# One set of 128 slots for two experts of different router groups, and eight landing slots for the weights

## The reference, cut to what matters

```python
N_GROUPS, EXPERTS_PER_GROUP, TOP_K, D_FF_EXPERT = 4, 4, 2, 512     # 16 experts

def moe(h2, router_w, router_b, w1, w3, w2):
    scores = jax.nn.sigmoid(h2 @ router_w)
    biased = (scores + router_b).reshape(n_tok, N_GROUPS, EXPERTS_PER_GROUP)
    group_score = jnp.sum(lax.top_k(biased, 2)[0], axis=-1)
    gidx = jnp.argmax(group_score, axis=-1)            # one group for each token
    _, loc = lax.top_k(in_group, TOP_K)                # two experts of that group
    eid = gidx[:, None] * EXPERTS_PER_GROUP + loc
    gates = sel / jnp.sum(sel, axis=-1, keepdims=True)
    ...
    y = (jax.nn.silu(xb @ w1[e]) * (xb @ w3[e])) @ w2[e]     # for the tokens of expert e
    return y * g[:, None]                                    # and summed back to the tokens
```

## Time and profile before

| | |
|---|---|
| median of 3 runs | 2137.87 us (2137.78 to 2141.77) |
| the profiled execution | 2146.0 us, span 2144.2 us |
| granted TensorE clock, mean | 0.952 |
| PE busy | 93% of the span |
| DVE, ACT busy | 67%, 53% |
| read from memory | 454.35 MB, 212 GB/s over the span |
| first mixture layer | about 250 to 608 us of the span |
| second mixture layer | about 753 to 1110 us of the span |

### The profile page before, as it was taken

The page is one execution under the profiler, slowest core; times in us unless marked ns, Lnnn a source line. Parts: engine busy times, 40 slices in busy tenths (PEclk is TensorE's granted clock), DMA queues, the critical chain, the costliest instruction groups (busy, mean ns, idle before and its releaser), DMA issues.

```text
span 2144.2 us, 28128 instructions
## 1 busy us (share of the span) xinstructions
PE 1995.2 (93%) x11557; PEld 1698.1 (79%) x11557; DVE 1431.9 (67%) x1851; ACT 1136.8 (53%) x1499; POOL 79.6 (4%) x84
## 2 busy tenths in 40 slices
PE   4984899999989899999979999989999999989998
PEld 2843688888767678888869998779999998778997
DVE  2666588888776588888866555656556556666555
ACT  3332477676657467676745445535344443645433
POOL 0000001000000010010000000000000000000000
PEclk8987899999989899999989999979999999989999
DMA  8563688888759558787855555325555555424552
GB/s 319 197 229 144 216 294 293 296 294 295 275 181 322 205 199 307 282 307 283 305 200 177 183 190 192 118 80 180 193 181 175 195 179 191 156 80 152 181 194 91
DMA packets 209328, 457.33 MB, mean 213 GB/s; under 512 B 8848, under 2 KB 20776, under 8 KB 209192
## 3 DMA queue, kind: packets, MB, share of 16 engines
q1 hardware_dynamic: 204800, 450.99, 60.1%
q10 hardware_dynamic: 4392, 4.44, 0.6%
HBM read 454.35 MB, written 1.05 MB: 212 GB/s over the span
## 4 chain that ended last, share of the span: by engine, by line
PE 87%; DVE 6%; ACT 4%; DMA 2%; issue 1%; POOL 0%; SPq 0%; ACTq 0%; DVEq 0%; POOLq 0%
PE bank L290 84%; PE bank L1906 2%; DVE arena L1206 2%; DVE rest L618 1%; DMA raw<-in_mod_w 1%; ACT round L601 1%; PE bank L2165 1%; DVE arena L1198 1%; ACT arena L727 0%; DMA raw<-in_ev_out_w 0%; DMA raw<-in_od_in_w 0%; DVE acc L1198 0%; DVE xres L1198 0%; PE bank L2147 0%; DVE htokl L1198 0%
## 5 line engine op out<-in xcount | busy, mean ns | idle before, releaser
L618 DVE TENSOR_TENSOR rest<-raw,round 128x1024 fp32r<-128x1024 f32 (+1 forms) x760 | 889.7, 1217 | 266.3 <-ACT round L601 265.5
L601 ACT ACTIVATE round<-raw 128x1024 fp32r<-128x1024 f32 (+1 forms) x760 | 758.6, 1050 | 415.1 <-PE bank L290 389.4
L290 PE MATMUL bank<-hTh,round 128*128 128x256 f32 x1600 | 451.0, 282 | 15.2 <-DVE hTl L1198 12.8
L290 PE MATMUL bank<-hTh,rest 128*128 128x256 f32 x1600 | 449.9, 281 | 0.0
L290 PE MATMUL bank<-hTl,round 128*128 128x256 f32 x1600 | 448.7, 280 | 0.0
L290 PEld LDWEIGHTS bank<-hTh,round 128*128 128x128 f32 x1600 | 302.6, 189 | 21.6 <-issue 20.9
L290 PEld LDWEIGHTS bank<-hTl,round 128*128 128x128 f32 x1600 | 303.7, 190 | 1.1 <-issue 0.2
L290 PEld LDWEIGHTS bank<-hTh,rest 128*128 128x128 f32 x1600 | 303.2, 189 | 0.0
L290 PE MATMUL bank<-round,hTh 128*128 128x512 f32 x464 | 188.1, 405 | 6.5 <-DVE hTl L1198 2.9
L290 PE MATMUL bank<-rest,hTh 128*128 128x512 f32 x464 | 184.2, 397 | 0.0
L290 PE MATMUL bank<-round,hTl 128*128 128x512 f32 x464 | 184.1, 397 | 0.0
(11 more groups left out here) (219 smaller groups left out, 2543.4 us busy)
## 6 DMA issues: line engine op xcount, KB each, us to landing
raw<-in_ex_w SPq DMA_DIRECT2D x192, 1024.0 KB, 5.6
raw<-in_mod_w SPq DMA_DIRECT2D x48, 1024.0 KB, 7.3
raw<-in_ffn_w_gate SPq DMA_DIRECT2D x44, 1024.0 KB, 5.0
raw<-in_ffn_w_up SPq DMA_DIRECT2D x44, 1024.0 KB, 5.0
raw<-in_ffn_w_down SPq DMA_DIRECT2D x44, 1024.0 KB, 4.8
raw<-in_w_in SPq DMA_DIRECT2D x20, 1024.0 KB, 5.0
raw<-in_ev_in_w SPq DMA_DIRECT2D x10, 1024.0 KB, 9.9
raw<-in_od_in_w SPq DMA_DIRECT2D x8, 1024.0 KB, 5.3
```

Source lines behind the costliest of these rows:

```text
L290: return e.matmul(o, l, r, start=start, stop=stop, skip_group_check=True)
L601: e.activation(hi[:, h], raw[:, h], ACT.Copy).then_inc(S("hi"), 1)
L618: e.tensor_tensor(lo[:, h], raw[:, h], hi[:, h].bitcast(F32), ALU.subtract).then_inc(S("lo"), 1)
```

## The change

The 16 experts form 8 pairs: (0,4), (1,5), (2,6), (3,7), (8,12), (9,13), (10,14), (11,15). Both experts of a pair share one set of 128 slots: the places of the second expert's tokens follow those of the first. So there is one one-hot matrix for a pair, and one gather brings the tokens of two pairs (four experts). Each expert's first and third product run over all 128 slots of the pair; the gate of each slot for each of the two experts, which is zero for the tokens of the other one, is multiplied into the hidden rows (DVE, in the same instruction as before, with one more operand). Then the down products of both experts add up in the same two banks, and are taken out and scattered once for both. The work of an expert other than that stays as it is, and so does the order within PE's work, up to what the diff shows. `NSLOT` goes from 6 to 8. To make room, `acc` and the temporary of the residual move into the arena, `muf` into `rows`, and the parameters of the gating unit into `gbc`. The flag now asks for more than 128 tokens in a pair.

```diff
-NSLOT = 6
+NSLOT = 8
...
+PAIRS = [(8 * h + j, 8 * h + j + 4) for h in range(2) for j in range(4)]
+NP = len(PAIRS)
+NQ = NP // 2
...
     def moe(l):
-        for e in range(NE):
-            by_cols("ex_w1", (l, e), D, 0, 512)
-            if 0 < e < NE - 1:
-                by_rows("ex_w2", (l, e - 1), 0, 4)
-            by_cols("ex_w3", (l, e), D, 0, 512)
-        by_rows("ex_w2", (l, NE - 2), 0, 4)
-        by_rows("ex_w2", (l, NE - 1), 0, 4)
+        for p in range(NP):
+            a, b = PAIRS[p]
+            by_cols("ex_w1", (l, a), D, 0, 512)
+            if p:
+                for ex in PAIRS[p - 1]:
+                    by_rows("ex_w2", (l, ex), 0, 4)
+            by_cols("ex_w3", (l, a), D, 0, 512)
+            by_cols("ex_w1", (l, b), D, 0, 512)
+            by_cols("ex_w3", (l, b), D, 0, 512)
+        for ex in PAIRS[-1]:
+            by_rows("ex_w2", (l, ex), 0, 4)
...
-                ts(place, place, -1.0, None, ALU.add).then_inc(S("place"), 1)
+                pp4 = pp.rearrange("p (h j) -> p h j", j=4)
+                stt(pp4, member(place, 4, 0), -1.0, member(place, 4, 1), ALU.add, ALU.add).then_inc(S("place"), 1)
...
+                def gated(p, m):
+                    e.wait_ge(S("moe_silu"), 16 * l + 2 * p + m + 1)
+                    e.wait_ge(S("used"), W.last("ex_w3", (l, PAIRS[p][m]), 0) + 1)
+                    e.wait_ge(S("gate_hot"), NP * l + p + 1)
+                    stt(muf[0:CAP, :], muf[0:CAP, :], gg[0:CAP, 2 * p + m:2 * p + m + 1], banks[1][0:CAP, :], ALU.mult, ALU.mult
+                        ).then_inc(S("moe_u"), 1)
...
+                def down(p, between=None):
+                    e.wait_ge(S("ug_lo"), 16 * l + 2 * p + (2 if between is None else 1))
+                    for m, ex in enumerate(PAIRS[p]):
+                        if m and between is not None:
+                            e.wait_ge(S("ug_lo"), 16 * l + 2 * p + 2)
+                        for r in (0, 2):
+                            i, k, views = take("ex_w2", (l, ex), r * 128, 0)
+                            for nh, b in enumerate((2, 3)):
+                                for f in (r, r + 1):
+                                    ins = mm3(e, banks[b][0:CAP, :], [x[:, f, :] for x in ug[m]],
+                                              [x[:, f - r, nh * 512:(nh + 1) * 512] for x in views],
+                                              m == 0 and f == 0, m == 1 and f == 3)
+                                if m and r == 2 and nh == 0:
+                                    ins.then_inc(S("y_0"), 1)
+                            ins.then_inc(S("used"), 1)
+                            if m == 0 and r == 0 and between is not None:
+                                between()
...
+                for p in range(NP):
+                    q = p // 2
...
+                    def in_b1():
+                        if p:
+                            e.wait_ge(S("yg_lo"), 2 * (NP * l + p))
+                        turn_hidden(p, 0, 2)
+
+                    def in_b3():
+                        if q + 1 < NQ:
+                            e.wait_ge(S("ug_lo"), 16 * l + 2 * p + 1)
+                            gather(q + 1, p % 2, (2, 3))
...
+                    rows_times("ex_w1", p, 0, 0, in_a1)
...
+                    turn_hot(p)
+                    if p:
+                        down(p - 1)
+                    e.wait_ge(S("gate_hot"), NP * l + p + 1)
+                    rows_times("ex_w3", p, 0, 1)
+                    e.wait_ge(S("moe_silu"), 16 * l + 2 * p + 1)
+                    rows_times("ex_w1", p, 1, 0, in_b1)
+                    if p:
+                        scatter(p - 1)
+                    rows_times("ex_w3", p, 1, 1, in_b3)
+                down(NP - 1, lambda: turn_hidden(NP - 1, 1, 0))
+                scatter(NP - 1)
```

More of the change, by code:

```diff
@@ L411, in program @@
         c_mx = c2["mix"].rearrange("p (l k) -> p l k", l=2)
-        xn = region(12288, 2, D)
+        xn, tmps, acc = region(4096, 2, D), region(6144, 2, D), region(0, 2, D)
         hf = region(10240, KC, T)
@@ L444, in program, with of_pair, member @@
         v8 = lambda a: a.rearrange("p (g n) -> p g n", g=8)
-        mask, place, late, gg = (ms[:, 32 * i:32 * i + 32] for i in range(4))
-        muf = region(13056, 512)
+        mask, place, late = (ms[:, 32 * i:32 * i + 32] for i in range(3))
+        gg, pp = ms[:, 96:112], ms[:, 112:128]
+        def of_pair(a, p):
+            return a[:, 8 * (p // 4):8 * (p // 4) + 8].rearrange("p (b j) -> p b j", b=2)[:, :, p % 4]
+        def member(a, n, b):
+            return a.rearrange("p (h b j) -> p h b j", h=n, b=2)[:, :, b, :]
+        muf = rows[:, :, :].rearrange("p a b -> p (a b)")
         m_u, m_g = region(0, 2, 512), region(1024, 2, 512)
@@ L883, in hidden, with down @@
+                def hidden(p, m, b):
+                    e.wait_ge(S("hid_T"), 16 * l + 2 * p + m + 1)
+                    e.activation(ug[m][0].rearrange("p f c -> p (f c)"), banks[b][:, 0:4 * CAP], ACT.Copy
                                  ).then_inc(S("ug_hi"), 1)
-                def down(ex):
-                    at = W.where["ex_w2", (l, ex), 256, 0]
-                    for nh, b in enumerate((2, 3) if ex < NE - 1 else (1, 0)):
+                def down(p):
+                    at = W.where["ex_w2", (l, PAIRS[p][1]), 256, 0]
+                    for nh, b in enumerate((2, 3)):
@@ L919, in moe @@
-                ends = [W.where["ex_w2", (l, ex), 256, 0] for ex in (NE - 2, NE - 1)]
+                for p in range(NP):
+                    a, b = PAIRS[p]
+                    a1, a3, b1, b3 = (W.last(n, (l, ex), 0) for ex in (a, b) for n in ("ex_w1", "ex_w3"))
+                    act_split(e, ahead, a1 - 1)
+                    if p:
+                        hidden(p - 1, 1, 2)
+                        act_split(e, ahead, a1)
+                        act_split(e, ahead, a1 + 1)
+                    silu(p, 0)
+                    e.wait_ge(S("hot_turned"), NP * l + p + 1)
+                    e.activation(GT[p % 2][0:CAP, :, :].rearrange("p a b -> p (a b)"), banks[1][0:CAP, 0:256], ACT.Copy
+                                 ).then_inc(S("hot_T"), 1)
+                    if p:
+                        for i in range(a1 + 2, a1 + 5):
+                            act_split(e, ahead, i)
+                        down(p - 1)
+                    else:
+                        act_split(e, ahead, a1)
+                    for i in range(a3 - 1, b1):
+                        act_split(e, ahead, i)
+                    hidden(p, 0, 2)
+                    act_split(e, ahead, b1)
+                    act_split(e, ahead, b3 - 1)
+                    silu(p, 1)
+                    act_split(e, ahead, b3)
+                    if p // 2 + 1 < NQ:
+                        gathered(p // 2 + 1, p % 2, (2, 3))
@@ L920, in moe @@
+                ends = [W.where["ex_w2", (l, ex), 256, 0] for ex in PAIRS[-1]]
                 act_split(e, ahead, ends[0] - 1)
-                hidden(NE - 1, 0)
+                hidden(NP - 1, 1, 0)
                 act_split(e, ahead, ends[0])
-                down(NE - 2)
                 act_split(e, ahead, ends[1] - 1)
                 act_split(e, ahead, ends[1])
-                down(NE - 1)
+                down(NP - 1)
                 overflow(l)
```

276 lines of the change are left out of this document (122 added, 154 removed).

## The result

The changed kernel takes 2040.59 us (median of 4 runs, 2037.56 to 2044.79), the kernel before beside it 2139.82 us. The ratio is 0.9535, 95% interval 0.9515 to 0.9556. That is 99 us less, where 83 were predicted, and 1.4 us under the lower end of the range.

A forecast was written before the change was run, and what follows sets the result against it. PE was taken as the limit, with no wait left in an expert; 65.4 + 12.3 + 5 = 82.7 us off the median of 2137.9 gave 2055 us (chance 0.70), own range 2049 to 2063, with rivals 2042 to 2083.

The forecast's parts named there:

- The moved buffers: `acc`, `muf` and `xn` in new places: same number of instructions and same place in the engines' order, no cost.
- What is removed, 65.4 us: Mixture layers: 8 fewer half gathers, scatters and `turn_hot` each, priced at full PE spacing; 32.7 us a layer, 65.4 both.
- the last expert's wait with the clock behind it: Expert 15, both layers: PE's 3.33 us wait for DVE's gate sum goes, with 2.75 and 2.91 us of low clock; 12.3 us.
- The pair: A pair of experts in a mixture layer goes from 42.80 to 38.7 us, PE busy throughout at clock 1.00.
- Eight slots, 5 us: Odd stage: two more weight pieces fetched ahead bring everything behind 5 us earlier; bounds 0 and about 11 us.
- ACT's waits under 8 us: Sign to look for in the odd stage: ACT's waits for transfers, 15.9 us before, under 8 us together.
- Even mixer and the start of a layer, 0: No gain from ACT's 4.60 us wait for ev_out_w (bound 4.6), nor from PE asking 1.91 us earlier at a layer's start.
- Short waits in each pair (2): Splits or hidden product late by about 1.5 us in each pair, 24 us in all: 2079 us; chance 0.15.
- The transfers (3): Weight transfers become the limit in the pairs: 2085 us at 310 GB/s, 2120 at 295; chance 0.05.
- The wait with the low clock in each pair (5): One wait per pair long enough to lower PE's clock, 6.1 us each, 98 us in all: 2153 us; chance 0.02.
- the slow path (6): The change fails its purpose and the flag for too many tokens in a pair starts it: over 2140 us; chance 0.01.
- Rival 4: Slots give more: both odd-stage waits and the even mixer's vanish whole, about 11 + 3 instead of 5: 2046 us; chance 0.07.

The follow-up runs named there:

- after_pad128: Changed kernel with 128 bytes left free ahead of the landing slots, moving slots and rounding buffers; 2058.28 us, ratio 0.9616.
- pad128: Kernel before with 128 bytes left free ahead of the landing slots, moving slots and rounding buffers; 2121.97 us, ratio 0.9904.
- early_gates: Kernel before with the sum of the gates at expert 15 ahead of the next piece's split, on DVE and ACT; 2133.26 us, ratio 0.9971.
- gather2: Changed kernel with each half gather inside the loop over pairs done twice; 2064.54 us, ratio 0.9628.
- pad_rounds: Kernel before with 128 bytes left free behind the slots, so only the rounding buffers move; 2112.13 us, ratio 0.9879.
- pairs6: Changed kernel with six slots in place of eight; 2042.52 us, ratio 0.9549.

## Why the prediction was wrong, step by step

**The step that failed** is the sentence "The moved buffers (`acc`, `muf`, `xn`) keep their number of instructions and, by the order of the engines, their place. No cost." It priced the move by the instructions on the moved buffers alone. But taking `acc` out of the front and shortening the arena also shifts everything allocated behind them, the slots and rounding buffers, through which every split weight goes to PE. The term is not 0 but -17.7 us (`after_pad128` to the changed kernel), and -19.6 us in the kernel before (`pad128`). It acts on some 9,000 matmuls on weights, 2 to 4 ns each, most of them outside the changed code; the distances of the table would make it some 25 us between the two paired kernels, so the sizes agree only to several us.

**With this term taken out the sum comes out within the noise.** `after_pad128` is the changed kernel without the lucky shift. It takes 2058.28 us, 83.2 less than the kernel before beside it (78 to 87 by the interval), where the sum had 82.7. That the two agree to half a microsecond is luck. The stages of its profiled execution against those of before, which has the same distances, and of the other kernels:

| profiled execution | up to layer 0 | layer 0 | odd stage | layer 1 | rest | span |
|---|---|---|---|---|---|---|
| before | 250.5 | 358.2 | 145.5 | 356.1 | 1033.9 | 2144.2 |
| `after_pad128` | 244.2 | 319.6 | 139.2 | 317.2 | 1034.8 | 2054.9 |
| `pad128` | 249.0 | 354.2 | 142.1 | 350.8 | 1024.6 | 2120.6 |
| `early_gates` | 244.8 | 353.1 | 143.6 | 350.8 | 1035.3 | 2127.5 |
| `gather2` | 246.5 | 327.4 | 141.4 | 325.3 | 1025.2 | 2065.8 |

- **What is removed, 65.4 us, and the last expert's wait with the clock behind it, 12.3 us.** The two layers lose 38.6 and 38.9 us, 77.5 in all, for 77.7 reckoned. The first term is also tested by `gather2` (11.3 and 11.5 us a layer for 11.5), the second by `early_gates` (5.1 and 5.3 us with 0.95 us of wait left in each, for 6.1 and 6.2). Both read it against the same execution of the kernel before, which had the largest fall of the clock of the five kernels with this wait; the prediction took that fall as certain, and `pad_rounds` shows the same wait with none. The waits are 6.7 us in every execution; what the clock adds is 0 to 3 us a layer.
- **The pair.** Reckoned 38.7 us; at the distances of before it is 38.64, as the window over a pair of `after_pad128` shows, with 327 GB/s where 325 were reckoned:

```profile
287.76:326.40 38.64, 38.64 (x181) 31.65 (x180) 33.03 (x34) 28.26 (x33) 6.64 (x4) 1.00 0.92 327
```

- **Eight slots, 5 us.** The mechanism at the transfers was right (ACT's waits under 8 us: 2.0), the size isn't shown: 2.2 and 1.9 us in two comparisons whose intervals don't exclude 5, both with the weights' buffers on the multiple of 256. In one profile each, `after_pad128` has an odd stage 6.3 us shorter than before, the changed kernel one 2.8 shorter; but that stage takes 139.2 to 145.5 us in the fourteen profiles, at a mean granted clock of 0.85 to 0.90, so one profile each doesn't price the slots. What the traces do show is that PE kept 2.2 us of the 6.3 by which it comes to `mrow` earlier. The prediction didn't ask what is late next: ACT's copy of `mrow`, 3.96 us, with its own fall of the clock.
- **Even mixer and the start of a layer, 0.** Nothing in the traces speaks against it; the time up to layer 0 is 243 to 253 us in the fourteen profiles, in no order of kernels, so a change of 2 us there would not be seen.
- **The rivals.** Short waits in each pair (2) did not come: PE has no wait inside the pairs; the spare half microsecond was enough. The transfers (3) did not bind: 25 us windows of the changed kernel's mixture layers go up to 370 GB/s. The wait with the low clock in each pair (5) and the slow path (6) did not come. Rival 4, more from the slots, gives 2046 us and would have been the nearest number, but for a reason that the experiments don't bear out: the waits for transfers went, and 2 us came of it.

Rival 5's rule, "TensorE: Matmul & The Clock Gate" of the Trainium skill under "HAM oscillation", is that an engine which waits between bursts pays the return to the full clock each time. The traces here agree only in part. The waits of 3.33 and 3.96 us above had the lower clock behind them (0.65, 0.64, 0.52), that of 0.95 us had not (1.00); but neither had the 3.33 us of `pad_rounds`, and the kernel before has the lower clock behind a wait of 1.50 us in the odd stage, where `pairs6` has none behind one of 2.02 us:

```profile
697.73 0.47 PE L290 MATMUL bank<-round,catTh 128*128 128x512 f32 x1 [1.50 <-DVE rest L618]
```

```profile
699.10:702.30 3.20, 3.20 (x9) 2.45 (x8) 1.52 (x2) 3.19 (x5) 0.00 (x0) 0.50 1.06 390
```

```profile
660.01:665.81 5.80, 5.80 (x25) 4.78 (x26) 3.79 (x5) 2.96 (x3) 0.00 (x0) 1.00 0.92 345
```

The first two are of the kernel before, the last of `pairs6`. So the length of a wait alone doesn't tell what the clock does behind it, and a rival of one wait per pair could not be priced from one such wait.

**What stays open** is why the places matter (that the load of the next stationary operand meets the running matmul's reads is a guess that no run tests), and why 128x256 has two levels within one kernel when both buffers are on the multiple. The activations' buffers `hT`, `catT` and `uT` were not moved in any run, so it isn't shown whether the starts count by themselves or by their distance from those buffers; and offsets other than 0, 64 and 128 weren't tried.

## What to carry to other kernels

A change of the memory layout shifts every buffer allocated behind it. Where PE is the limit, write down the start of each operand that PE reads, before and after, and if it differs, run the old kernel with a pad that gives it the new starts: only against that one can a change in the program be priced. And where a transfer's wait is removed, follow the engine that is the limit up to its next wait before you count the gain: here two waits for split weights, 4.1 us together, became one of 3.96 us for another engine. And where a price has a fall of the clock in it, read that fall in more than one execution.

## What the runs showed of the hardware that was not expected

- The distance of matmul starts at the full clock depends on where the buffers start: with slots and rounding buffers both 64 or 128 bytes off a multiple of 256, 232.4 to 233.2 ns for 128x512 and 117.3 to 118.8 for 128x256; otherwise 229.5 to 231.1 and 113.6 to 115.8. In the stretches shown above, both kinds on the multiple against both 128 off, the two differ by 4.3 ns at either size. In this kernel that is 18 to 20 us, 0.9%. "TensorE: Matmul & The Clock Gate" of the Trainium skill (section "Wait — 56ns, not 53.3ns?") has the column count through 2.4 GHz and about 2.5 ns more, which gives, as an estimate, 215.8 and 109.2 ns; the traces stand 13 to 18 and 4 to 10 ns above it, and show a dependence that this sum has no term for.
- The same page of the Trainium skill (section "Step-by-step: what each phase is for") says that a load of weights has a read port of its own and takes nothing from the running matmul. No run here shows the ports; but that the place of the buffers read changes the distance is something that this rule alone doesn't lead one to expect.
- Two executions of one and the same kernel can have the same stage at either level (117.7 and 113.5 ns).
- The same wait of PE, 3.33 us at the same place of the program, is followed by 24 matmuls in 8.35 us at a granted clock of 0.65 in the kernel before and in 5.63 us at 1.00 in `pad_rounds`.
